# A ring of weight slots made two slots shorter

## The reference

```
x = first_block(x, c, ctx, ...)     # adaLN modulation, w_in (1024 x 6656), retention with a
                                    # context state, Hyena long convolution by DFT, w_out,
                                    # then a mixture of experts: 4 groups x 8 experts, top 2,
                                    # y = (silu(u @ w1[e]) * (u @ w3[e])) @ w2[e], hidden 512
return second_block(x, c_2, ctx_2, ...)
# second_block, for each of two layers: adaLN modulation, w_in_2 (1024 x 2304),
#   Fourier mixing, neighbourhood attention, spatial gating, differential attention,
#   w_out_2, then square(relu(h @ w_ff1_2)) @ w_ff2_2 with 4096 hidden columns;
#   the context stream of layer 0 goes through the same layer
```

## Time and profile before

| | |
|---|---|
| runs, us | 1820.09, 1821.25, 1824.27 |
| profiled execution, us | 1820.09, its span 1818.3 |
| PE busy | 1763.6 us, 97% of the span |
| DVE, ACT busy | 462.9 us (25%), 324.5 us (18%) |
| read from HBM | 470.29 MB, 259 GB/s over the span |
| granted clock of TensorE | 0.996 of full |

### The profile page before, as it was taken

How to read it: one execution, slowest core, us unless ns; L and a number is a source line. 1 busy time by engine, 2 the same in 40 slices (tenths; PEclk the granted TensorE clock), 3 DMA queues, 4 the chain that set the end, 5 groups by cost and what they waited for, 6 DMA issues and landing times. The chain is left out here.

```text
span 1818.3 us, 24604 instructions
## 1 busy us (share of the span) xinstructions
PE 1763.6 (97%) x10866; PEld 1343.3 (74%) x10866; DVE 462.9 (25%) x1010; ACT 324.5 (18%) x732; POOL 0.2 (0%) x4
## 2 busy tenths in 40 slices
PE   6999999999999999999999999999999999999997
PEld 4674887888664566676767587688888876888886
DVE  5310124525115220111101154531100135411001
ACT  4110013203214111010000124521100135211000
POOL 0000000000000000000000000000000000000000
PEclk9999999999999999999999999999999999999999
DMA  9552687466999999999999973374444231554410
GB/s 378 226 227 106 264 324 281 187 239 261 378 388 416 412 421 421 421 421 420 421 421 421 422 297 143 117 270 170 152 149 161 93 116 46 230 190 159 147 61 23
DMA packets 61810, 472.93 MB, mean 260 GB/s; under 512 B 7719, under 2 KB 11208, under 8 KB 12040
## 3 DMA queue, kind: packets, MB, share of 16 engines
q1 hardware_dynamic: 60472, 470.08, 65.5%
q10 hardware_dynamic: 1232, 1.28, 0.2%
HBM read 470.29 MB, written 1.05 MB: 259 GB/s over the span
## 5 line engine op out<-in xcount | busy, mean ns | idle before, releaser
L2520 PE MATMUL bank<-hT,ring 128*128 128x256 f32 x1024 | 221.5, 379 | 0.0
L2539 PE MATMUL bank<-second_work,ring 128*128 128x256 f32 x1024 | 221.3, 379 | 0.0
L2539 PEld LDWEIGHTS bank<-second_work,ring 128*128 128x128 f32 x1024 | 194.6, 190 | 26.5
L2520 PEld LDWEIGHTS bank<-hT,ring 128*128 128x128 f32 x1024 | 194.4, 190 | 26.4
L1345 PE MATMUL bank<-hT,ring 128*128 128x256 f32 x704 | 160.5, 385 | 4.2 <-issue 2.8
L1345 PEld LDWEIGHTS bank<-hT,ring 128*128 128x128 f32 x704 | 132.9, 192 | 38.6 <-issue 16.2
L650 PE MATMUL bank<-hT,ring 128*128 128x256 f32 x704 | 153.9, 379 | 0.0
L650 PEld LDWEIGHTS bank<-hT,ring 128*128 128x128 f32 x704 | 133.5, 191 | 18.8 <-issue 1.2
L1813 PE MATMUL bank<-ring,rowsT 128*32 128x512 f32 x1008 | 116.8, 596 | 0.1
L1345 PE MATMUL bank<-tmp,ring 128*128 128x256 f32 x384 | 86.5, 382 | 1.6 <-DMA ring<-in_w_out 0.8
L1345 PEld LDWEIGHTS bank<-tmp,ring 128*128 128x128 f32 x384 | 71.9, 190 | 20.3 <-issue 5.9
(11 more groups left out here) (468 smaller groups left out, 1704.8 us busy)
## 6 DMA issues: line engine op xcount, KB each, us to landing
ring<-in_expert_w SPq DMA_DIRECT2D x190, 1024.0 KB, 16.1
ring<-in_w_ff SPq DMA_DIRECT2D x96, 1024.0 KB, 7.2
ring<-in_ada_w SPq DMA_DIRECT2D x36, 2048.0 KB, 9.0
ring<-in_w_in SPq DMA_DIRECT2D x29, 1024.0 KB, 8.7
ring<-in_w_in SPq DMA_DIRECT2D x13, 2048.0 KB, 11.7
ring<-in_w_out SPq DMA_DIRECT2D x12, 1024.0 KB, 4.9
ring<-in_ret_w_o SPq DMA_DIRECT2D x2, 2048.0 KB, 7.7
ring<-in_w_out SPq DMA_DIRECT2D x2, 2048.0 KB, 9.9
```

What stands on the lines that cost most here:

```text
L2520: mm = pe.matmul(ff_bank(n), w[:, k, (n % 2) * P:(n % 2 + 1) * P], hT[:, k, xs], start=k == 0, stop=k == DT - 1)
L2539: mm = pe.matmul(ff_bank(FT + i), w[:, f, :], W[:, 16 * h + f, :], start=h == f == 0, stop=h == 1 and f == FT // 2 - 1)
```

## The change

Two numbers. The ring has 8 slots instead of 10, and the descriptor space of transfers through GpSimd goes from 256 bytes in each partition to its default, 16384. The two slots are 16384 bytes in each partition.

```
-SLOTS = 10
+SLOTS = 8
...
-    nc = bacc.Bacc("TRN2", target_bir_lowering=False, num_devices=1, dynamic_dma_scratch_size=256)
+    nc = bacc.Bacc("TRN2", target_bir_lowering=False, num_devices=1)
```

## The result

The changed kernel takes 1833.49 us (median of its runs, 1831.10 to 1845.05) where the kernel before takes 1822.46 (1820.09 to 1824.27): ratio 1.0061, interval 1.0039 to 1.0083. It is slower, as forecast, but by twice the amount: 11 us instead of 5.3, and outside the range that ended at 1830.5.

What follows compares the result with a forecast made beforehand. It took the DMA engines, at 421 GB/s and a little slower than PE, to bound the expert stage. 4.98 + 0.3 = 5.3 us, put on the median of 1821.25, gave 1826.4 us, range 1822.8 to 1830.5.

Steps and rivals of the forecast that it cites:

- What bounds the kernel: From 605 to 1047 us the DMA engines, at 421 GB/s, are slower than PE by a little.
- The stock of landed loads: Expert stage: it shrinks by 2 MB and reaches zero well before 643 us, where PE then waits the 5 us.
- All waits of the stage: Sign: PE's waits for ring loads in the expert stage come near 10 to 11 us instead of 5.5.
- Two loads since the last dry point, +4.98: Expert stage: from 527.16 us to load 283 the DMA list is longer by loads 77 and 78, 4.98 us.
- Load 45, +0.3: Last ada_w load before the router: it waits for load 41, so PE waits 0 to 0.7 us, taken as 0.3.
- Start, rest and descriptor space, 0: Program start, loads outside the experts and the space for transfers through GpSimd: no change in time, 0 us.
- The rival that the start could be faster: Program start: four transfers held back let loads 1 to 3 land sooner, up to 11.1 us won, 1815.3 us; chance 0.03.
- More dry spells: Expert stage, behind 605 us: the queue runs out at two or three more places, +9 to +11, 1831 us; chance 0.10.
- The price per place: Expert stage: each further place where the queue runs out costs 1.7 to 2.0 us, like the dips at 500 and 530.
- GB/s under 415 in the expert stage: Sign that the forecast is wrong: a DMA rate this low in the expert stage would mean dry spells.

Runs made afterwards that it cites:

- e14: The kernel before, with load 103 alone also waiting for what it would wait for in a ring of 6 slots: 1829.51 us, ratio 1.0025.
- e6: The kernel before with its 10 slots, loads 58 to 102 also waiting as in a ring of 8: 1827.05 us, ratio 1.0019.
- e1: The kernel before with 8 slots instead of 10, its descriptor space left at 256: 1831.48 us, ratio 1.0039.
- e3: The kernel before with its 10 slots, loads 0 to 57 and from 284 on also waiting as in a ring of 8: 1823.66 us, ratio 1.0000.
- e5: A separate kernel of 1 MB loads alone, without the computation: 4.77 us from landing to landing with 1 under way, 2.48 to 2.49 with 4 or more.
- e12: The kernel before repeated unchanged, for a third profile of it: 1822.82 us (one run).

## Why the prediction was wrong

**What bounds the kernel: right.** e14 shows it: what the DMA engines lose once, at load 103, is still lost at load 283. The stock of landed loads also went as forecast: PE's first waits for loads come 20 us earlier than the 643 us of the earlier trace rows, between 605 and 643, and at its instruction of 643 us PE is 7.3 us late. All waits of the stage come to 12.9 us, where the forecast had 10 to 11. The first and the fourth of them in the changed kernel:

```profile
623.37 1.07 PE L1813 MATMUL bank<-ring,rowsT 128*32 128x512 f32 x8 [1.00 <-DMA ring<-in_expert_w]
...
650.71 3.72 PE L1345 MATMUL bank<-tmp,ring 128*128 128x256 f32 x16 [1.43 <-DMA ring<-in_w_out]
```

**Two loads since the last dry point, +4.98: nearly right.** Load 79 lags 5.8 us in the changed kernel, of which 0.5 is load 45. By itself (e6) the term is 4.9 us at load 102 and 3.4 at load 283, 4.1 with PE's early start taken off. One reading was off at no cost: at 527.16 us the queue was not empty, load 78 landed 2.3 us later; load 79 still took 2.6 us more than its 2.49.

**Load 45, +0.3: right.** It is issued at 430.02, takes 8.4 us and PE waits 0.5, inside the 0 to 0.7 of the forecast; in the other profiles with this limit PE falls 0.1 to 0.5 us behind there. By the Trainium skill ("DMA: Bandwidth & Descriptors", the anatomy of one DMA) an estimate for 2 MB is 6.8 us, and the term nothing. The section gives its fit for transfers issued by GpSimd; this one, issued by SP, took 8.4, so the fit doesn't serve here.

```profile
438.50 1.95 PE L386 MATMUL bank<-ring,cond_pair 128*32 128x128 f32 x64 [0.51 <-DMA ring<-in_ada_w]
```

**Start, rest and descriptor space, 0: right.** PE is within 0.9 us of its old times in the first 36 us and within 0.03 us from there up to load 44, though loads of that part land later, load 12 by 11 us and load 9 by 25: they are still early. The rival that the start could be faster falls too: load 1 lands 0.7 us earlier, load 2 0.6 later. e1 takes the descriptor space out, e3 the start and the end.

**"More dry spells", given 0.10: this is what happened, and rejecting it was the step that failed.** The prediction said: "behind 605 us the shortest queue is 5.0 us shorter. The shortest there is at 887.79 ...; 0.7 is left", and "Against: it is above zero, and the places are few". Three things in it are wrong. The step at fault is "5.0 us shorter", a transfer time put where PE's reading time belongs: 5 us is the mean of two loads' reading (4.9), but PE's reading is uneven, and at the tight places the queue got 6 to 15 us shorter. So the shortest place before was not the shortest after: load 222 went from 15.1 to 3.1, while load 224, the one of 887.79, went only from 8.2 to 7.2. And a queue need not be empty to cost: under 4 us each issue costs 0.6 to 1.8 us on the mean. Last, the forecast looked only behind 605 us. Two of the six low issues, loads 103 and 104, are ahead of it (595.96 and 597.33 us), where before had load 105 with 3.9 us left. (PE is 1.5 us later there by a stretch at the lower clock at 589 us, which the first profile of before doesn't have; without it loads 103 and 104 would have had 3.3 and 5.1 us left.)

The price per place, 1.7 to 2.0, was too high, and the number of places, two or three, too low; six issues at 3.5 us together took their stead. The rest of the 4.4 us between loads 103 and 283, 0.9, is within what single profiles of one kernel scatter; on the mean of three profiles the 4.4 are 3.2. That this rival's sum, +9 to +11, meets the 11 us measured is luck in part: 2.0 of them are the clock's, which it did not have.

**The clock: a term that the forecast did not have.** 2.0 us behind load 283 (2.1 and 1.4 in the repetitions), of open cause.

The sum of the profile: 0.5 (load 45) + 4.4 (lag at load 102, less that) + 4.4 (loads 103 to 283) + 2.0 (clock) = 11.3 us, beside 11.0 between the two profiled executions. By the signs that the prediction set itself, "GB/s under 415 in the expert stage" was to mean dry spells; 417 came. The sign was set too coarse: over 442 us one GB/s in 421 is a whole us.

## What to carry to other kernels

When buffers are taken from a prefetch ring, don't subtract the transfer time of the lost buffers from the queue. For each load, look up when the consumer releases the buffer that it would then wait for, and compare that moment with the landing of the load ahead of it; do it at every load, because the tight places of the shorter ring are others than those of the longer one. The trace of the longer ring is enough for it: with two slots fewer, the queue left at load n is about the landing of load n - 1 less the issue of load n + 2. Done so for the loads from 112 on, the first profile of before gives nine places under 4 us, the lowest 3.2 us at load 222. In the changed kernel these nine have 3.1 to 5.2 us left, and the four under 4 us are among them. (The rule takes the landings and PE to be equally late. From load 112 on they differ by 0.9 us on the mean; at loads 103 and 104 they differ by 2.9 and 3.6 us, and there it gives -1.1 and 0.0 us where 1.8 and 3.6 were left.)

Count a place as at risk when under about 4 us (here one and a half loads of 1 MB) are left, not only when nothing is; and where the transfers are the bound, expect each loss to stay to the end of the stage, as it did here.

## What the runs showed of the hardware

- On one queue, loads of 1 MB follow each other every 4.77, 3.37, 2.53 and 2.49 us with 1, 2, 3 and 4 under way (e5). With 2 under way they alternate, 2.4 to 2.6 and 3.5 to 4.6 us.
- The kernel before is not as steady as its fastest run. In its third profile (e12) PE runs at the lower clock at 573 us, reads its loads 2.7 us late, and so frees slots late; load 105 is issued with 1.2 us left, where the first profile had 3.9, and load 283 lands 2.7 us later. The run took 1822.82 us, not 1820.09. Around 572 us, e12 first, then the first profile of before:

```profile
572.00:580.00 8.00, 8.00 (x37) 2.64 (x36) 1.85 (x6) 3.05 (x11) 0.00 (x0) 0.57 1.02 424
```
```profile
572.00:580.00 8.00, 7.89 (x61) 2.69 (x59) 4.27 (x13) 4.66 (x17) 0.00 (x0) 1.00 1.01 422
```

  So a stretch at the lower clock far ahead of the end can reach the end by way of the slots that it frees late. Thirteen of the sixteen profiles have a stretch at the lower clock between 571 and 593 us, whatever their ring; the first profile of before is one of the three without. It may be a part of why the medians of the short and the long ring stand 7 to 11 us apart in different rounds; that is not shown.
- The Trainium skill ("DMA: Bandwidth & Descriptors", "Where 436 GB/s comes from") gives HBM's limit for a core as about 358 GB/s, half of what two cores have together. With one core running it did not bind: the changed kernel keeps 417 GB/s over 453 us, and loads alone run at 421 (1.0486 MB in 2.49 us). No run here has a second core at work.
